# Input weights in column groups that later tensors move into, and queries stored in two parts

## The chip, the cores and the metric

One core of one Trainium2 chip runs the whole program as one launch. The metric is the device time of one execution in microseconds (us); lower is better. TensorE (PE) does matrix products, VectorE (DVE), ScalarE (ACT) and GpSimd (POOL) do elementwise work, and SyncE (SP) mostly issues DMAs. Each engine runs its own instructions in order and waits on semaphores.

## The reference

One mixer layer over 2048 new frames (16 tiles of 128) and 32 frames of a running stream (a 17th tile with 1024 cached keys), d_model 1024:

```
proj = RMSNorm(x) * g_pre @ w_in          # 2600 columns: u, gate_a, q, k, v, qi, ki, wi, gate_b
pool branch: (mean_window(u) - u) -> per-group linear -> scale, times silu(gate_a)
score = sum_h wi * relu(qi . ki)          # indexer; the 256 best visible keys of each query are kept
logits = q . k / 8 + rel_bias[bucket(distance)]; o = softmax over kept keys @ v, times silu(gate_b)
y = x + RMSNorm([pool | o] @ w_out) * g_post
```

## The kernel before, in words

The program has two phases, each one block in which every engine has its own stream, with a barrier between them. SBUF tensors of phase 1 are freed before those of phase 2 are allocated, so phase 2 loads what it needs after the barrier.

**Phase 1.** `phase1_steps` (L86) writes out one order of steps that all engines walk through. Tokens come in blocks of 4, 4, 4, 2 and 3 tiles. For each tile: N (norm of x), H (transposes into `hT`), TM (the token-major product of k, v, qi, ki, wi: 552 columns), and for each block 16 feature-major products of 128 columns each: GB (gate_b), Q, GA (gate_a), U, for four groups g. After a U come PD and PL (window means on GpSimd, difference on VectorE, a product, a VectorE multiply at L1014). TR transposes keys and index queries. I steps are pieces of the indexer scores, spread between the products; SP steps are pieces of a binary search on VectorE. The input weights `W` are one tensor [128, 8, 2600], loaded in 16 DMAs of whole row parts (L491, L493) and multiplied by g_pre on VectorE (L910) in two lots: the columns from K on when the third tile is normed, the first 1536 columns when step TM of tile 0 comes up. Three DMAs of zeros (L498) blank the end of scratch tensors in DRAM.

The relative bias is a table `G` of 8 heads (8 partitions) by 895 distances. ScalarE's queue writes it to DRAM at step TR of tile 0 (L670), 128 times over for each head, so that phase 2 can read it back with a skew as `EB` [128, 8, 768]. In phase 1 nothing but the end of the phase waits for that write (`bias_out`). ScalarE copies every product out of PSUM (fa banks 0 and 1 in turn, bank 2 for the gates, bank 3 for transposes); Q is copied with its scale and stored to `q_scratch` (L706, L563). PE needs a bank freed before it starts the product after next on it.

**Phase 2.** For each tile t, PE computes maxima products M of tile t+1 (L1473), logits A of tile t (L1486 to L1491: high part of q, low part of q, mask, shift), the weighted values two jobs behind (L1506), and the output projection O of tile t-1 (L1521: 8 products with `ma` first, then 8 with `yT`). Queries are loaded as one f32 tile (four DMAs, L1257); ScalarE rounds the high part `qh` (L1375), GpSimd subtracts to get the low part `ql` (L1315), and only then is the buffer free for the next load. ScalarE also does 16 search rounds for tile t+3 and VectorE 10 more for tile t+2, besides VectorE's maxima. SP walks its own loop over t: gb(t), mask(t+3) (tiles 3 to 5: waits for all logits of tile t), S(t+4), ma(t), q(t+2), y(t-2), xr(t-1).

Of the kernel before, what the change touches and what calls it, by code (L numbers as in the profile page):

```python
# [26 lines left out]
P = 128  # L27
D = 1024
# [19 lines left out]
COLS = 2600  # L48
BIAS_TILES = 6
# [36 lines left out]
def phase1_steps():  # L86


    steps = [("N", 0), ("N", 1), ("N", 2)]
# [34 lines left out]
    for b, (t0, nt) in enumerate(BLOCKS):  # L124
        last = b == len(BLOCKS) - 1
        ahead = [] if last else list(range(t0 + nt, t0 + nt + min(3, BLOCKS[b + 1][1])))
        todo = [(k, b, g) for g in range(NG) for k in ("GB", "Q", "GA", "U")]
        for i in range(nt):
            t = t0 + i
            if i == 0:  # L130
                for j in range(nt):
                    steps.append(("H", t0 + j))
                    spread(1)
                    seek()
                    if j == 0 and nt == 4:
                        steps.append(("N", t0 + 3))
                if last:
                    steps.append(("HIST",))
# [4 lines left out]
            project(("TM", t), 1 + sum(taking))  # L143
            pool_part()
            cached = 0 <= t - 4 < PAST // P
            for j, step in enumerate(mine):
                if step[0] != "Q":
# [3 lines left out]
                if step[0] == "U":  # L151
                    windows.append(step[1:])
                if j < 3:
# [22 lines left out]
    steps += [("NP", 0), ("NP", 1)]  # L176
# [29 lines left out]
def build(nc, A):  # L206
    ctx = ExitStack()
    with ctx:
# [8 lines left out]
        def dram(name, shape, dt=F32):  # L217
# [3 lines left out]
        q_dram = dram("q_scratch", (P, GRP, TOKENS))  # L221
# [11 lines left out]
        k2 = [sb(ctx, f"k2_{kv}", [P, SEQ], F32R) for kv in range(NKV)]  # L233
        unit = sb(ctx, "unit", [P, NT], F32)
# [4 lines left out]
        phase1(nc, A, sb, sem, identf, identb, onesb, k2, unit, banks, wide, q_dram, gb_dram, ma_dram, s_dram, m_dram,  # L239
               g_dram, k_dram)  # L240
        phase2(nc, A, sb, sem, identf, identb, onesb, k2, unit, banks, wide, q_dram, gb_dram, ma_dram, s_dram, m_dram,
               g_dram, k_dram)

# [106 lines left out]
def phase1(nc, A, sb, sem, identf, identb, onesb, k2, unit, banks, wide, q_dram, gb_dram, ma_dram, s_dram, m_dram,  # L350
           g_dram, k_dram):
# [5 lines left out]
    with ExitStack() as st:  # L357
        W = sb(st, "W", [P, DC, COLS], F32)
# [23 lines left out]
        qst = sb(st, "qst", [P, 2, 512], F32)  # L382
        U = sb(st, "U", [P, NG, UOFF + 512], F32)
# [3 lines left out]
        rows = sb(st, "rows", [HIST, 3, DPOOL], F32)  # L387
# [10 lines left out]
        wa_in = [sem(f"wa_in{c}") for c in range(DC)]  # L398
        wb_in = [sem(f"wb_in{c}") for c in range(DC)]
# [3 lines left out]
        w_scaled = sem("w_scaled")  # L403
# [13 lines left out]
        gst_out = [sem(f"gst_out{i}") for i in range(2)]  # L417
# [1277 lines left out]
```

## Time and profile before

| | us |
|---|---|
| median of 3 runs | 1875.71 (1874.71 to 1877.98) |
| the profiled execution | 1873.14 |
| its span, first to last instruction | 1871.3 |
| PE / DVE / ACT / POOL busy | 1619.6 / 1246.7 / 905.4 / 437.2 |
| granted PE clock, mean | 0.945 |

The page cuts the span into 40 slices; each digit is the busy share in tenths. Phase 1 is the first 18 to 19 slices, phase 2 the rest. A slice is 46.8 us.

```
PE   2999899979888798886487899899999999999996
DVE  3212656677676865764233899999999999885412
ACT  2112223233323334542127899888888887633331
PEclk9999899999999899988598899999999999999998
DMA  8350201020111011003712221112210110101000
```

### The profile page before, as it was taken

How to read it: one execution, taken by the hardware profiler on the slowest of the kernel's cores; microseconds unless marked ns; L12 is line 12 of the kernel's file. 1: busy time of each engine (PE TensorE's matmuls, PEld its weight loads, DVE VectorE, ACT ScalarE, POOL GpSimd, SP SyncE). 2: the span in 40 equal slices, each digit the busy share in tenths (PEclk: the TensorE clock that was granted, in tenths of full speed). 3: DMA queues.
4: the chain of work that ended last, by engine and by line, in shares of the span. 5: the costliest groups of instructions: out<-in, count | busy, mean ns of one | idle time of the engine just before them, and what ended most of it. 6: DMA issues, size and time to landing. Idle time of an engine off the chain costs nothing.

```text
span 1871.3 us, 17741 instructions
## 1 busy us (share of the span) xinstructions
PE 1619.6 (87%) x5191; PEld 892.3 (48%) x5191; DVE 1246.7 (67%) x3000; ACT 905.4 (48%) x1681; POOL 437.2 (23%) x341
## 2 busy tenths in 40 slices
PE   2999899979888798886487899899999999999996
PEld 1545555545444577664243444444444444454542
DVE  3212656677676865764233899999999999885412
ACT  2112223233323334542127899888888887633331
POOL 0000100010000101001243454434433334332342
PEclk9999899999999899988598899999999999999998
DMA  8350201020111011003712221112210110101000
GB/s 318 63 73 30 70 34 40 34 77 33 37 49 44 35 42 36 30 35 92 232 38 94 74 68 61 41 46 65 67 40 29 58 40 6 42 4 46 29 29 17
DMA packets 85587, 107.39 MB, mean 57 GB/s; under 512 B 17158, under 2 KB 64838, under 8 KB 85363
## 3 DMA queue, kind: packets, MB, share of 16 engines
q1 hardware_dynamic: 80330, 101.54, 16.3%
q10 hardware_dynamic: 5160, 4.71, 2.1%
q8 instruction: 42, 0.69, 0.2%
q14 instruction: 55, 0.44, 0.1%
HBM read 67.15 MB, written 39.09 MB: 57 GB/s over the span
## 4 chain that ended last, share of the span: by engine, by line
PE 22%; DVE 19%; issue 5%; ACT 3%; POOL 2%; DMA 1%; SPq 1%; POOLq 0%; DVEq 0%; ACTq 0%
PE wide L1521 7%; PE wide L1506 6%; DVE above L306 6%; DVE max_junk L1584 3%; DVE den L1599 2%; PE bank L1486 2%; PE bank L1487 2%; PE bank L1488 2%; POOL E L1365 2%; PE bank L1491 2%; PE bank L1473 1%; DVE S L340 1%; ACT act_junk L1415 1%; DMA q<-q_scratch 1%; DVE reach L344 1%
## 5 line engine op out<-in xcount | busy, mean ns | idle before, releaser
L785 PE MATMUL bank<-hT,W 128*128 128x512 f32 (+2 forms) x1280 | 490.2, 526 | 1.5 <-ACT kq L699 1.0
L1365 POOL TENSOR_TENSOR E<-E,EB 128x512 f32<-128x512 f32 x174 | 255.9, 1474 | 465.5 <-ACT E L1448 465.2
L785 PEld LDWEIGHTS bank<-hT,W 128*128 128x128 f32 x1280 | 243.9, 197 | 173.8 <-issue 150.7
L1448 ACT ACTIVATE E<-bank 128x512 f32<-128x512 f32 x290 | 171.7, 592 | 259.0 <-PE bank L1491 258.1
L1506 PE MATMUL wide<-E,vx 128*128 128x512 f32 x544 | 285.2, 606 | 4.0 <-POOL E L1365 4.0
L1415 ACT ACTIVATE act_junk<-S,minus_cand 128x1152 bf16<-128x1152 f32 (+9 forms) x165 | 246.3, 1493 | 2.4
L765 ACT ACTIVATE relu<-wide 128x1024 f32<-128x1024 f32 (+7 forms) x192 | 153.3, 803 | 184.5 <-PE wide L800 129.2
L1045 DVE SCALAR_TENSOR_TENSOR S<-relu,wi,S 128x1024 f32<-128x1024 f32 (+7 forms) x168 | 170.0, 1012 | 81.8 <-ACT relu L765 74.3
L1584 DVE CUSTOM_DVE_ANT_0 max_junk<-bank,mask 128x512 bf16<-128x512 f32 (+3 forms) x230 | 136.7, 613 | 103.7 <-PE bank L1473 78.3
L306 DVE TENSOR_SCALAR_CACHE_REDUCE above<-S,search 128x1152 bf16<-128x1152 f32 (+9 forms) x110 | 188.2, 1711 | 0.8
L1473 PE MATMUL bank<-k,qh 128*128 128x512 f32 (+3 forms) x214 | 143.5, 688 | 40.6 <-DVE mxp L1584 25.6
L1521 PE MATMUL wide<-wout,ma 128*128 128x512 f32 x272 | 145.6, 629 | 24.3 <-ACT osb L1441 17.0
L1486 PE MATMUL bank<-qh,k 128*128 128x512 f32 x272 | 158.4, 582 | 4.7 <-issue 2.6
L1521 PE MATMUL wide<-wout,yT 128*128 128x512 f32 x272 | 142.6, 622 | 15.4 <-POOL yT L1327 15.4
L638 POOL TENSOR_TENSOR win<-U 128x512 f32<-128x512 f32 (+11 forms) x20 | 19.0, 951 | 580.5 <-ACT U L717 580.5
L800 PE MATMUL wide<-kiT,qiT 96*128 96x512 f32 (+3 forms) x304 | 138.0, 525 | 16.2 <-ACT relu L765 16.2
L785 PE MATMUL bank<-W,hT 128*128 128x296 f32 (+1 forms) x544 | 146.2, 409 | 2.5 <-ACT hT L686 2.5
L1506 PEld LDWEIGHTS wide<-E,vx 128*128 128x128 f32 x544 | 105.0, 194 | 47.0 <-POOL E L1365 7.9
L785 PEld LDWEIGHTS bank<-W,hT 128*128 128x128 f32 x544 | 105.7, 197 | 31.1 <-issue 7.6
L1488 PE MATMUL bank<-identb,mask 128*128 128x512 bf16 x290 | 115.4, 398 | 0.0
L1491 PE MATMUL bank<-shift,onesb 128*128 128x512 bf16 x290 | 112.5, 388 | 0.0
L1487 PE MATMUL bank<-ql,k 128*128 128x512 f32 x272 | 109.6, 403 | 0.0
(183 smaller groups left out, 2128.7 us busy)
## 6 DMA issues: line engine op xcount, KB each, us to landing
q<-q_scratch SPq DMA_DIRECT2D x68, 128.0 KB, 2.9
xs<-x_prompt SPq DMA_DIRECT2D x16, 512.0 KB, 4.2
xr<-x_prompt SPq DMA_DIRECT2D x16, 512.0 KB, 5.3
y_prompt<-osb SPq DMA_DIRECT2D x16, 512.0 KB, 3.6
W<-w_in SPq DMA_DIRECT2D x8, 768.0 KB, 17.5
s_scratch<-S SPq DMA_DIRECT2D x11, 512.0 KB, 2.6
gb<-gb_scratch SPq DMA_DIRECT2D x17, 256.0 KB, 5.5
ma<-ma_scratch SPq DMA_DIRECT2D x17, 256.0 KB, 4.8
```

What stands on the lines that cost most here:

```text
L306: dve.tensor_scalar((B.above, B.reach)[i][:, 0:s.shape[1]], s, B.cand[:, i:i + 1], None, ALU.is_ge, ALU.add, accum_out=B.cnt[:, i:i + 1]). ...
L765: act.activation(relu[:, k % 2, 0:b - a], wide[k % 2][:, 0:b - a], ACT.Relu)\
L785: mm = pe.matmul(out, stationary(c), moving(c), start=(c == 0), stop=(c == DC - 1))
L1045: dve.scalar_tensor_tensor(row, relu[:, k % 2, 0:b - a], w, row, ALU.mult, ALU.add)\
L1365: pool.tensor_tensor(E[:, k % 4], E[:, k % 4], EB[:, kv * GRP:(kv + 1) * GRP, off:off + P], ALU.mult)\
L1415: act.activation(act_junk[:, 0:w], S[:, sslot(u), 0:w], ACT.Sign, bias=minus_cand[:, u % 2:u % 2 + 1], accum_out=act_sum[:])\
L1448: act.activation(E[:, k % 4], banks[2 + k % 2][:].rearrange("p (j n) -> p j n", j=GRP), ACT.Exp).then_inc(fl_free, 1)
L1473: pe.matmul(max_banks[k % 3][:, 0:b - a], qh[:, t % 2, kv, j, :], keys[:, a:b], start=True, stop=True)\
L1486: pe.matmul(bank, keys, qh[:, t % 2, kv], start=True, stop=False)
L1506: pe.matmul(wide[0][:, kv * 512:(kv + 1) * 512], values[:, kt, kv:kv + 2, :].rearrange("p a d -> p (a d)"), E[:, k % 4].rearrange("p j n - ...
L1521: mm = pe.matmul(wide[1][:, 0:512], stat, wout[:, c, i * 512:(i + 1) * 512], start=(c == 0), stop=(c == DC - 1))
L1584: dve.tensor_tensor_reduce(junk[:, k % 2, 0:b - a], max_banks[k % 3][:, 0:b - a], mask[:, t % 3, a:b], 1.0, LEAST, ALU.add, ALU.max, mxp[: ...
```

## The change

It has these parts.

1. `w_in` is laid out by the host as 16 column groups of 128 columns (each [128 partitions, 8 x 128]) and one group TM of 552 columns. On chip they lie in one tensor `home`, which both phases share. Loads: x(0), small tables, TM in 8 DMAs with x(1) between, x(2), 16 group DMAs of 512 KB with x(3) after the second. g_pre is applied to TM right after the norm of tile 0 (step WT), and to each group by one tensor-tensor multiply (step WG), one after each H of block 0 and two ahead of each product.
2. TM of tile 0 comes right behind H of tile 0, ahead of H of tiles 1 to 3.
3. `G` has no tensor of its own: it lies in `sga`, the buffer of the gate_a results. So ScalarE's first GA step waits for the write of `G` to DRAM.
4. Q: ScalarE writes the rounded high part, VectorE the low part (`qlow`), and both are stored. The bank is freed by VectorE; ScalarE waits for that before its next fa copy.
5. In the last block the order of products is U and GA of all groups first, then GB and Q. As groups of `home` are used up, `EB`, `vx`, the first `S` and half of `w_out` are loaded into them while phase 1 still runs. The NP steps move up behind the last block's first GB.
6. Phase 2 loads high and low parts as they are (eight DMAs a tile, three and two buffers), and ScalarE's and GpSimd's query steps are gone. SP's loop for t from 1 on is: gb(t), mask(t+3), high(t+2), low(t+1), and at t = 1 g_post and two S tiles, then S(t+4), ma(t) and the rest.

```diff
-    steps = [("N", 0), ("N", 1), ("N", 2)]
+    steps = [("N", 0), ("WT",), ("N", 1), ("N", 2)]
...
                     steps.append(("H", t0 + j))
+                    if b == 0 and j == 0:
+                        project(("TM", 0), 0)
...
+                    if b == 0:
+                        scale(1)
...
             for j, step in enumerate(mine):
+                scale(2)
...
-        G = sb(st, "G", [NH, GLEN], F32)
+        G = sga[:].rearrange("p a n -> p (a n)")[0:NH, 0:GLEN]
...
+                    elif s == ("Q", last_block, 2):
+                        sp.wait_ge(fa_full, fa["Q", last_block, 1] + 1)
+                        sp.wait_ge(fg_full, fg["GB", last_block, 1] + 1)
+                        sp.dma_start(home[:, 8 * GROUP:12 * GROUP], A["w_out"][:, 0:4 * GROUP])\
+                          .then_inc(loaded["wout_in"], 16)
...
                             dst = sga[:, m % 2, 0:T]
+                            if m == 0:
+                                act.wait_ge(bias_out, 16)
...
-                        act.activation(qst[:, n % 2, 0:T], banks[k % 2][:, 0:T], ACT.Copy, scale=ATTN_SCALE)\
-                           .then_inc(fa_free, 1)
+                        act.activation(qst[:, n % 2, 0:T].bitcast(F32R), banks[k % 2][:, 0:T], ACT.Copy, scale=ATTN_SCALE)\
+                           .then_inc(q_high, 1)
...
+                    elif s[0] == "WG":
+                        k = scaled_at[s[1:]]
+                        group = WG[s[1:]]
+                        dve.wait_ge(wg_in[k - 1], 16)
+                        dve.tensor_tensor(group, group, gpre[:].rearrange("p (c n) -> p c n", n=1)
+                                          .broadcast_to([P, DC, P]), ALU.mult).then_inc(wg_scaled, 1)
...
+                    elif s[0] == "Q":
+                        k, n_q, T = fa[s], q_slot[s], width(s[1])
+                        dve.wait_ge(q_high, n_q + 1)
+                        if n_q:
+                            dve.wait_ge(qlow_out, 16 * n_q)
+                        dve.scalar_tensor_tensor(qlow[:, 0:T], banks[k % 2][:, 0:T], ATTN_SCALE,
+                                                 qst[:, n_q % 2, 0:T], ALU.mult, ALU.subtract).then_inc(fa_free, 1)
...
                     load_mask(t + 3)
+                    if t >= 1:
+                        load_high(t + 2)
+                        load_low(t + 1)
+                    if t == 1:
+                        sp.dma_start(gpost[:], A["g_post"].broadcast_to([P, D])).then_inc(gpost_in, 16)
+                        load_S(FIRST + 1)
+                        load_S(FIRST + 2)
```

## Rows read from the trace of the kernel before

**Rows 1.** Windows: us, then busy us (count) by engine, PEclk, DMA share, GB/s.
```profile
20.00:40.00 20.00, 2.54 (x11) 1.74 (x9) 9.03 (x24) 0.95 (x2) 0.00 (x0) 1.00 1.01 362
60.00:80.00 20.00, 20.00 (x56) 9.39 (x55) 3.87 (x14) 4.39 (x10) 0.00 (x0) 1.00 0.43 55
...
900.00:920.00 20.00, 8.79 (x19) 4.63 (x20) 4.72 (x25) 2.14 (x3) 4.84 (x3) 0.50 1.04 352
1070.00:1110.00 40.00, 35.97 (x106) 17.13 (x105) 38.71 (x90) 36.81 (x79) 19.20 (x14) 0.96 0.28 83
```

**Rows 2.** Timeline of the start: start us, us, engine, line, what.
```profile
3.36 0.42 SPq L488 DMA_DIRECT2D relb<-rel_bias  x1
...
18.63 1.94 PE L818 MATMUL bank<-identf,xs 128*128 128x128 f32 x8 [6.79 <-DVE xs L930]
...
23.97 5.55 DVE L910 TENSOR_SCALAR W<-W,gpre 128x1064 f32<-128x1064 f32 x8
...
47.79 7.68 PE L785 MATMUL bank<-W,hT 128*128 128x256 f32 x32 [0.78 <-ACT hT L686]
...
55.31 7.03 PE L785 MATMUL bank<-hT,W 128*128 128x512 f32 x16
```

**Rows 3.** Timeline, the bias table's write and the tanh ahead of it.
```profile
62.37 0.60 ACT L733 ACTIVATE gst<-bank 128x512 f32<-128x512 f32 x1 [6.45 <-PE bank L785]
62.38 1.28 ACTq L670 DMA_DIRECT2D bias_scratch<-G  x1
```

**Rows 4.** DMA queues: packets, MB, share of 16 engines, in 64:66, 66:68, 140:141.
```profile
q10 hardware_dynamic: 27, 0.10, 46.0%
...
q10 hardware_dynamic: 29, 0.10, 49.4%
...
q10 hardware_dynamic: 1, 0.00, 0.1%
```

**Rows 5.** DMA issues in 60:150: what, count, KB each, us to landing.
```profile
gb_scratch<-gst SPq DMA_DIRECT2D x3, 256.0 KB, 22.7
```

**Rows 6.** Timeline, ScalarE's copies after U of block 0 and in TM of tile 1.
```profile
84.18 0.60 ACT L717 ACTIVATE U<-bank 128x512 f32<-128x512 f32 x1 [6.23 <-PE bank L785]
...
87.64 0.38 ACT L699 ACTIVATE kq<-bank 128x256 f32<-128x256 f32 x1 [2.86 <-PE bank L785]
```

**Rows 7.** Waits of PE, 60:870: who for whom, us in total, times, longest.
```profile
PE bank L860 <- DVE gst L1014: 35.2, 14, 5.9
```

**Rows 8.** Timeline of the end of phase 1.
```profile
862.10 7.92 PE L785 MATMUL bank<-hT,W 128*128 128x288 f32 x32
...
875.99 0.35 SPq L557 DMA_DIRECT2D ma_scratch<-gst  x1
878.61 2.58 SPq L1257 DMA_DIRECT2D q<-q_scratch  x4
```

**Rows 9.** Waits in 868:950, in total.
```profile
ACT qh L1375 <- DMA q<-q_scratch: 43.5, 3, 17.7
```

**Rows 10.** Timeline of the start of phase 2.
```profile
889.38 0.69 PE L1473 MATMUL bank<-k,qh 128*128 128x128 f32 x2 [14.04 <-ACT qh L1375]
...
919.29 2.04 PE L1521 MATMUL wide<-wout,ma 128*128 128x512 f32 x2 [7.22 <-DMA ma<-ma_scratch]
...
948.32 0.33 SPq L1248 DMA_DIRECT2D mask<-mask_scratch  x1
...
953.73 0.79 PE L1486 MATMUL bank<-qh,k 128*128 128x512 f32 x1
...
957.45 1.10 PE L1521 MATMUL wide<-wout,ma 128*128 128x512 f32 x2 [1.38 <-ACT osb L1441]
```

**Rows 11.** One line's durations: ns min/median/max, first to last start.
```profile
L1315 POOL TENSOR_TENSOR ql<-q,qh x17: 2335/2353/2368, 889.4 to 1757.9; 128x1024 fp32r<-128x1024 f32 x17
...
L1594 DVE TENSOR_SCALAR shift<-identb,nmax x136: 240/249/1325, 892.6 to 1774.4; 128x128 bf16<-128x128 bf16 x136
...
L996 DVE SCALAR_TENSOR_TENSOR gst<-gst,bank x4: 687/687/689, 63.0 to 176.7; 128x512 f32<-128x512 f32 x4
```

More of the change, by code:

```diff
@@ L48 @@
 COLS = 2600
+BASE = {"GB": C_GB, "Q": C_Q, "GA": C_GA, "U": C_U}
+FIRST_ORDER = [(kind, g) for g in range(4) for kind in ("GB", "Q", "GA", "U")]
+LAST_ORDER = [(kind, g) for g in range(4) for kind in ("U", "GA")] + [(kind, g) for g in range(4) for kind in ("GB", "Q")]
+GROUP = DC * P
+TMW = C_GB - C_K
 BIAS_TILES = 6
@@ L86, in phase1_steps, with scale @@
 def phase1_steps():
-    steps = [("N", 0), ("N", 1), ("N", 2)]
+    steps = [("N", 0), ("WT",), ("N", 1), ("N", 2)]
+    unscaled = list(FIRST_ORDER)
+    def scale(n):
+        while unscaled and n:
+            steps.append(("WG", *unscaled.pop(0)))
+            n -= 1
     inside = {}
@@ L126, in phase1_steps @@
         ahead = [] if last else list(range(t0 + nt, t0 + nt + min(3, BLOCKS[b + 1][1])))
-        todo = [(k, b, g) for g in range(NG) for k in ("GB", "Q", "GA", "U")]
+        todo = [(k, b, g) for k, g in (LAST_ORDER if last else FIRST_ORDER)]
         for i in range(nt):
@@ L218, in dram @@
             return nc.dram_tensor(name, shape, dt, kind="Internal").ap()
-        q_dram = dram("q_scratch", (P, GRP, TOKENS))
+        q_dram = [dram(f"q_{part}_scratch", (P, GRP, TOKENS)) for part in ("high", "low")]
         gb_dram = dram("gb_scratch", (P, GRP, TOKENS))
@@ L347, in choose, with homes, load_q_tile, phase1 @@
     return n
-def phase1(nc, A, sb, sem, identf, identb, onesb, k2, unit, banks, wide, q_dram, gb_dram, ma_dram, s_dram, m_dram,
-           g_dram, k_dram):
+def homes(home):
+    EB = home[:, 0:6 * GROUP].rearrange("p (h n) -> p h n", h=NH)
+    S0 = home[:, 6 * GROUP:8 * GROUP]
+    wout = home[:, 8 * GROUP:16 * GROUP].rearrange("p (c n) -> p c n", c=DC)
+    vx = home[:, 16 * GROUP:16 * GROUP + NPT * 3 * HD].rearrange("p (j a d) -> p j a d", j=NPT, a=3)
+    ma = home[:, 16 * GROUP + NPT * 3 * HD:16 * GROUP + NPT * 3 * HD + 2 * NG * P]\
+        .rearrange("p (i g n) -> p i g n", i=2, g=NG)
+    return EB, S0, wout, vx, ma
+def load_q_tile(sp, out, part, t, came):
+    for half in range(2):
+        for kv in range(NKV):
+            sp.dma_start(out[half * HD:(half + 1) * HD, kv], part[kv * HD:(kv + 1) * HD, :, t * P:(t + 1) * P])\
+              .then_inc(came, 16)
+def phase1(nc, A, sb, sem, identf, identb, onesb, k2, home, loaded, unit, banks, wide, q_dram, gb_dram, ma_dram,
+           s_dram, m_dram, g_dram, k_dram):
     steps, inside = phase1_steps()
@@ L437, in phase1 @@
         tm_order = {s[1]: i for i, s in enumerate(x for x in steps if x[0] == "TM")}
+        scaled_at = {part: k + 1 for k, part in enumerate(FIRST_ORDER)}
+        last_block = len(BLOCKS) - 1
         def width(b):
@@ L483, in _ @@
                 order = sorted(norm_order, key=norm_order.get)
-                for i in range(3):
-                    load_x(i, order[i])
+                load_x(0, order[0])
                 sp.dma_start(gpre[:], A["g_pre"]).then_inc(gpre_in, 16)
@@ L1387, in take_sums @@
                        .then_inc(sums_out, 1)
-                for kv in range(NKV):
-                    act.dma_start(vx[:, :, 2 * kv, :],
-                                  A["new_v_prompt"][0, 0, :, kv].rearrange("(j p) d -> p j d", p=P)).then_inc(v_in, 16)
-                high(0)
-                high(1)
                 def halved_by(t, r, part):
@@ L1453, in _ @@
                                 waiting.append((t, kv))
-                                if kv == NKV - 1 and t + 2 < NT:
-                                    high(t + 2)
                     if t == ST:
```

258 lines of the change are left out of this document (144 added, 114 removed).

## The prediction

> **What bounds the kernel now.** I read the page's slices first: PE is 87% busy and has two holes, the first slice and the 19th to 20th. The windows then give each stretch its limit. In 20 to 40 us PE works 2.5 of 20 us while the DMA engines are full at 362 GB/s; from the first products on it is full (20.00 of 20); in 900 to 920 it works 8.8 of 20 at a granted clock of 0.50 under a DMA share of 1.04; and in 1070 to 1110 VectorE is busy 38.7 of 40 and leads [rows 1]. So time is lost to weights at the start and to loads behind the barrier, and those two are what this change works on. Last I looked for what reads or writes the tensors that now share a place. There the table of biases stands out: its write is issued at 62.38 and its queue, q10, is still moving packets in the microsecond from 140 to 141 [rows 3, 4]. Nothing waits for it before. In the new kernel ScalarE does.
>
> **The start.** Before, the product TM of tile 0 starts at 47.79 and the first GB at 55.31 [rows 2]. New chain, by the same durations: the small table `relb` is issued behind one x tile, not three (two issues of 0.45 and 1 MB less ahead of it at some 360 GB/s [rows 1]), so everything up to the transposes of tile 0, which started at 18.63, comes 3.5 us earlier: 15.1. The eight TM scalings of 552 columns take half of the 5.55 for 1064 [rows 2], 2.9: 18.0. TM's 2.26 MB and two x tiles are 3.3 MB, 9 us of stream, landed by 14. TM of tile 0 takes 7.5 (47.79 to 55.31): 25.4. Then come VectorE's splits, the norm of tile 3 (2.8) and three rounds of transposes at 1.94 and a copy each, some 8 us together: the first GB starts at 33.3, 22.0 earlier. Its weights came long before and the scaling (16 multiplies at about 1.2, my estimate from 0.687 for 512 columns [rows 11]) runs ahead of PE. Up to here the change gains 22.
>
> **The new wait.** GB ends 22.0 earlier, so ScalarE issues the table's write at 40.4 instead of 62.38. Its rate is 27 packets in 2 us beside other stores and 29 alone [rows 4], 1024 rows of 3.6 KB in all: 71 to 76 us, and measured 77.8 from issue to the last packet. The share of 46 to 49% says eight of the sixteen engines carry it. It ends at 118.2. ScalarE reaches its first GA tanh at 54.5 and stands there, in order, with the copies of U and of TM of tile 1 behind it. PE runs on through U of group 0 and the first half of TM (to about 65.5) and then needs U's bank. After 118.2 come the tanh, a transposed copy and U's copy, 0.6 each [rows 3, 6]: PE goes on at 120.0 with TM's second half, which it started at 87.6 before [rows 6]. That is 32.4 late. PE has then idled 54 us; behind such a hole the clock was 0.50 for a while [rows 1], and I add 2.5 for half rate over some 5 us. **Start and wait together: +35.** The bounds are a write of 73 or 80 us and the first GB 3 us off: +28 to +41. The x tile for tile 4 queues behind the blanking and beside the table's packets (stores there took 22.7 to land [rows 5]), so it may come as late as 90; ScalarE is held anyway until 118. Were it later than 107, up to 11 would be added.
>
> The Trainium skill ("DMA: Bandwidth & Descriptors", Rules for kernel authors) says that an outermost dimension of fewer than 16 confines a DMA to that many engines at most. The table has 8 heads outermost and the trace agrees (46 to 49% of sixteen). By that rule nothing in the new layout speeds the write up; on all sixteen engines it would be 39 us shorter, and the forecast would be a gain.
>
> **Queries split in phase 1.** 20 VectorE subtracts: 12 at 0.69 and 8 shorter ones at about 0.45, 11.9 us in all [rows 11]. Until 190 us PE is full and they are hidden. After that PE waits for VectorE 14 times at a tile's transposes, 35.2 in all [rows 7], and there up to one subtract each can show. Both ends: 0 and 12; the bank that a Q now holds longer has 7 us of product between, so I take **+4**. The multiplies by g_pre are hidden by the stall.
>
> **The end of phase 1.** Before, the last product ends at 870.0 (862.10 + 7.92), and window, difference, product, multiply and store follow until 878.61 [rows 8], 8.6 us. Now a Q is last: copy 0.4, subtract 0.5, two issues 0.8, landing 1.7, barrier 0.9, some 4.8 with handovers. That is **-3.5**; the early loads (6.5 MB) run under the score pieces, and only the half of `w_out` can lie in front of the last store: -5 to +1.
>
> **The start of phase 2.** Let 0 be SP's first instruction, 878.61 before. The first maxima started at 10.8 (889.38) because ScalarE waited for the queries [rows 9, 10]; four DMAs at 0.64 and 2.8 of landing give 5.4. With no query step on ScalarE the first exponentials are not held up, and by the same durations the maxima of tile 1 end at 17.4, tile 1's logits start at 19.3. The first output product waited for `ma` until 919.29, at 40.7 [rows 10]; now 7.2 MB of that queue are loaded already, `ma` is issued at 17 behind 2.5 MB and is there at 22. From there to the end of tile 1's logits the work is the same chain, 26 us. That end was at 69.7 (mask issue 948.32 [rows 10]); now it is at 48: a gain of 21.5. Then something new is late. SP's mask for tile 4 waits for just this moment, and high(3) and low(2) are queued behind it: 0.3 + 2.6 + 2.6 of issue and 2.8 of landing, 8.3, where PE wants the low part after 5.4 (953.73); and `ma`, behind g_post and two S tiles, 13 to 14 us after, where it was wanted after 9.1 (957.45). That costs 4.5, and the same order for mask 5 costs 2 more one tile on. **-15**, between -8 (the waits twice as long) and -22 (no new wait).
>
> **The rest of phase 2.** ScalarE loses 17 roundings of 1.05, GpSimd 17 subtracts of 2.35 [rows 11]. VectorE leads here, and neither was in front of it in most tiles. But VectorE's 0.25 us shift rows reach 1.33 in places [rows 11], which I read as waiting for GpSimd. With some 0.5 us back in each of 12 tiles: **-6**; ends 0 and -28 (12 subtracts whole).
>
> **Sum** against the profiled execution: 1873.1 + 35 + 4 - 3.5 - 15 - 6 = 1887.6. The median is 2.6 above that execution, so I say 1889.
>
> **The rivals.**
> *VectorE gets GpSimd's time back* (ends faster). Each subtract that goes frees VectorE for its whole 2.35 us in the 12 tiles that it leads: -28 instead of -6, 1867. For: the rows of 1.33 against 0.25. Against: most shift rows are at the median, and a subtract need not meet a VectorE instruction that is kept out. It decides from 10 us beyond my 6 on, 1.3 us a tile.
> The Trainium skill ("SBUF — State Buffer", Who interferes with whom) calls the port pair of VectorE and GpSimd an exclusive lock, the later one blocked for a whole instruction. By that rule a tile could give back up to 2.35 us, the price above; the trace shows single rows five times their median, not that every subtract does it.
> *The wait costs nothing*: the write ends before ScalarE gets there, or PE finds other work. Then 22 us are gained at the start: 1873.1 - 22 + 4 - 3.5 - 15 - 6 = 1831, 1833 on the median. Against: the write would have to take 14 us, and PE's order is fixed.
> *VectorE is late in phase 1*: a subtract behind search rounds holds the bank, ScalarE's next copy waits for it and PE for that, at most of the 14 waits: +12 to +20 instead of +4, 1901. For: 5.9 us of such a wait once [rows 7]. Against: 7 us of product between.
> *The handover gives nothing*: new waits for low parts and `ma` eat the gain in phase 2: -3 instead of -15, 1901.
>
> **Chances.** Forecast 0.68, freed VectorE 0.10, no wait 0.08, late subtracts 0.08, no handover gain 0.06. The forecast's own range is 1877 to 1900. The range over all is 1867 to 1904: it leaves out the no-wait case and the tails. A difference of 0.2%, 3.7 us, is about what can be told from none. Faster: 0.08 + 0.08 + 0.02 of the forecast's tail = 0.18; the same: 0.01 + 0.07 = 0.08; slower 0.74.
>
> **What would show it.** The first 512-column product near 33; ScalarE idle from 55 to about 118 with the table's write as what ends it, and PE idle from 65 to 120; TM of tile 1 ending 33 to 36 later than at 91.4; that lag growing by under 8 until the last block; first maxima 5 to 6 us after SP's first instruction in phase 2; PE held at the first logits of tiles 2 and 3. I am wrong if ScalarE's wait ends before 100 or is absent, if the lag at 200 us is under 25, or if phase 2 is not 14 to 30 us shorter.

## The result, and the profile after

The changed kernel takes 1910.33 us (median of 4 runs, 1906.58 to 1912.48) against 1876.45 us (1874.71 to 1877.98) for the kernel before beside it: ratio 1.0187, 95% interval 1.0167 to 1.0207. It is slower, as forecast, but by 33.9 us and not 13, and outside the range that I gave (up to 1904). The profiled execution took 1908.91 us, 35.8 more than the one of before. Below, every ratio is to the kernel before, run beside that version, with a 95% interval in brackets. One execution of run 9 (1872.94 us) fell in a slower state than that kernel's others and is not counted.

The windows of the changed kernel (us, busy us and count of each engine, granted clock, DMA share, GB/s). Read them against [rows 1].

```profile
20.00:40.00 20.00, 16.54 (x60) 11.55 (x59) 14.22 (x45) 5.09 (x10) 0.00 (x0) 0.84 1.04 392
40.00:60.00 20.00, 20.00 (x52) 8.95 (x50) 1.12 (x2) 1.20 (x4) 0.00 (x0) 0.99 0.71 152
60.00:80.00 20.00, 13.45 (x37) 7.48 (x36) 7.63 (x17) 2.11 (x4) 0.00 (x0) 0.83 0.53 94
80.00:120.00 40.00, 0.00 (x0) 0.00 (x0) 0.00 (x0) 0.00 (x0) 0.00 (x0) 0.56 0.48 56
```

In 20 to 40 PE now works 16.5 of 20 us, where it worked 2.5. In 80 to 120 no engine does anything, while the DMA engines are 48% busy. The timeline of PE and ScalarE there, where [rows 2], [rows 3] and [rows 6] stood:

```profile
18.96 9.88 PE L890 MATMUL bank<-home,hT 128*128 128x256 f32 x32 [1.30 <-DVE home L1031]
...
36.42 9.10 PE L890 MATMUL bank<-hT,home 128*128 128x512 f32 x16 [0.78 <-ACT hT L786]
...
64.00 1.06 ACT L777 ACTIVATE junk<-xs 128x1024 bf16<-128x1024 f32 x1 [16.51 <-DMA xs<-x_prompt]
...
122.47 0.60 ACT L838 ACTIVATE sga<-bank 128x512 f32<-128x512 f32 x1 [56.36 <-DMA bias_scratch<-sga]
...
124.08 6.76 PE L890 MATMUL bank<-home,hT 128*128 128x296 f32 x16 [44.50 <-ACT U L820]
```

The first 512-column product starts at 36.42 instead of 55.31, and takes 9.10 us instead of 7.03 at a granted clock of 0.50 in 36 to 40 (the level of 1.2 GHz). The TM product of tile 0 takes 9.88 instead of 7.68. The windows print a clock of 1.00 there, but its first ten matmuls start 0.43 us apart and the next ones of the same width 0.22, so it too began at half the rate. ScalarE then stands 56.36 us before its first GA tanh, until the table has been written: issued at 45.57, waited for until 122.5, 76.9 us. Then it copies U and frees PE, which starts the second half of TM of tile 1 at 124.08 after 44.5 us of idleness. ScalarE's copy of the first half follows at 123.91, 36.3 later than at 87.64 [rows 6].

The last block of phase 1, rows of VectorE and then of PE:

```profile
877.37 1.22 DVE L1160 TENSOR_REDUCE small<-S 128x1 f32<-128x1024 f32 x1
878.51 1.21 DVE L1161 TENSOR_REDUCE small<-S 128x1 f32<-128x1024 f32 x1
...
880.32 0.51 DVE L1123 SCALAR_TENSOR_TENSOR gst<-bank,pscale,sga 128x288 f32<-128x288 f32 x1
```
```profile
880.88 1.03 PE L987 MATMUL bank<-identf,U 128*15 128x128 f32 x4 [4.79 <-DVE gst L1123]
...
884.50 1.09 PE L959 MATMUL bank<-identf,qs 128*96 128x128 f32 x4 [0.77 <-DVE rows L1089]
```

PE waits here for VectorE's multiply of step PL (L1123), which stands behind the sums and reductions of the indexer scores, and for the row copies of the NP steps (L1089). Over the whole last block its waits for that multiply add up to 19.3 us; in the kernel before they are 11.1. And the handover to phase 2, where [rows 8] and [rows 10] stood (the first row is SP's queue, the others PE; the last two views are PE's waits in 930 to 1060 and one row of the next tile):

```profile
933.55 2.57 SPq L390 DMA_DIRECT2D qh<-q_high_scratch  x4
```
```profile
938.40 0.69 PE L1560 MATMUL bank<-k,qh 128*128 128x128 f32 x2 [9.79 <-DMA qh<-q_high_scratch]
...
958.95 2.04 PE L1609 MATMUL wide<-home 128*128 128x512 f32 x2 [3.46 <-DMA home<-ma_scratch]
```
```profile
PE bank L1573 <- DMA ql<-q_low_scratch: 7.3, 2, 4.5
...
1038.58 0.79 PE L1573 MATMUL bank<-qh,k 128*128 128x512 f32 x1 [4.54 <-DMA ql<-q_low_scratch]
```

The first maxima start 4.85 us after SP's first instruction of phase 2, and PE then waits for low parts of the queries, which nothing did before.

To find where the 35.8 us go I follow one instruction per tile through both traces (VectorE's scaling of `wi` in TM of each tile, its reciprocal of each tile in phase 2) and take the lag, after less before:

```
TM of tile 1   tile 8   tile 14   tile 15   last product   SP phase 2   reciprocal 3   reciprocal 14   end
+39.3          +38.7    +43.9     +51.1     +58.6          +54.9        +49.8          +36.9           +35.8
```

| term | forecast | measured |
|---|---|---|
| start and wait | +35 | +39.3 |
| phase 1 from tile 1 to 14 | +4 (the split, whole phase) | +4.6 |
| last block of phase 1 | in the +4 | +14.7 |
| end of phase 1 | -3.5 | -3.7 |
| start of phase 2 | -15 | -5.1 |
| rest of phase 2 | -6 | -14.0 |

### The profile page after: what moved, and what is told of

The parts are those of the page before. It is cut to its first block, busy times and chain, and to the rows that moved or that the text cites. A ratio compares the mean times of both kernels' runs of the same rounds, so it can differ in the third digit from the quotient of the medians.

```text
span 1907.1 us, 17837 instructions
## 1 busy us (share of the span) xinstructions
PE 1624.9 (85%) x5143; PEld 897.3 (47%) x5191; DVE 1250.3 (66%) x3028; ACT 889.3 (47%) x1664; POOL 404.3 (21%) x324
## 3 DMA queue, kind: packets, MB, share of 16 engines
q10 hardware_dynamic: 1032, 3.67, 1.7%
## 4 chain that ended last, share of the span: by engine, by line
PE 20%; DVE 17%; issue 4%; ACT 4%; POOL 2%; another core or an unknown queue 2%; SPq 1%; DMA 0%; POOLq 0%; DVEq 0%; ACTq 0%
PE wide L1593 6%; PE wide L1609 6%; DVE above L329 5%; DVE max_junk L1672 3%; PE bank L1573 2%; PE bank L1575 2%; PE bank L1574 2%; ACT act_junk L1504 2%; DVE den L1687 1%; PE bank L1578 1%; POOL E L1466 1%; PE bank L1560 1%; SPq L390 1%; DVE reach L367 1%
## 5 line engine op out<-in xcount | busy, mean ns | idle before, releaser
L890 PE MATMUL bank<-hT,home 128*128 128x512 f32 (+2 forms) x1280 | 498.7, 534 | 6.9 <-DVE sga L1098 4.8
L1466 POOL TENSOR_TENSOR E<-E,home 128x512 f32<-128x512 f32 x174 | 256.7, 1479 | 497.6 <-ACT E L1537 497.5
L890 PEld LDWEIGHTS bank<-hT,home 128*128 128x128 f32 x1280 | 247.2, 200 | 184.4 <-issue 160.4
L1593 PE MATMUL wide<-E,home 128*128 128x512 f32 x544 | 282.4, 601 | 6.8 <-POOL E L1466 4.2
L890 PE MATMUL bank<-home,hT 128*128 128x296 f32 (+1 forms) x544 | 150.6, 418 | 47.5 <-ACT U L820 44.5
L1609 PE MATMUL wide<-home 128*128 128x512 f32 x272 | 144.8, 626 | 22.5 <-ACT osb L1530 15.4
L1504 ACT ACTIVATE act_junk<-S,minus_cand 128x1152 bf16<-128x1152 f32 (+5 forms) x105 | 155.3, 1479 | 1.4
L1609 PE MATMUL wide<-home,yT 128*128 128x512 f32 x272 | 139.7, 611 | 15.9 <-POOL yT L1432 15.9
L890 PEld LDWEIGHTS bank<-home,hT 128*128 128x128 f32 x544 | 108.1, 202 | 77.9 <-ACT U L820 44.9
L329 DVE TENSOR_SCALAR_CACHE_REDUCE above<-S,search 128x1152 bf16<-128x1152 f32 (+5 forms) x70 | 118.6, 1694 | 0.5
```

The source lines that it names most:

```text
L329: dve.tensor_scalar((B.above, B.reach)[i][:, 0:s.shape[1]], s, B.cand[:, i:i + 1], None, ALU.is_ge, ALU.add, accum_out=B.cnt[:, i:i + 1]). ...
L890: mm = pe.matmul(out, stationary(c), moving(c), start=(c == 0), stop=(c == DC - 1))
L1466: pool.tensor_tensor(E[:, k % 4], E[:, k % 4], EB[:, kv * GRP:(kv + 1) * GRP, off:off + P], ALU.mult)\
L1504: act.activation(act_junk[:, 0:w], S[sslot(u)][:, 0:w], ACT.Sign, bias=minus_cand[:, u % 2:u % 2 + 1], accum_out=act_sum[:])\
L1593: pe.matmul(wide[0][:, kv * 512:(kv + 1) * 512], values[:, kt, kv:kv + 2, :].rearrange("p a d -> p (a d)"), E[:, k % 4].rearrange("p j n - ...
L1609: mm = pe.matmul(wide[1][:, 0:512], stat, wout[:, c, i * 512:(i + 1) * 512], start=(c == 0), stop=(c == DC - 1))
```

## The experiments

Lags are against the profiled kernel before, as above.

**1. The table in a tensor of its own** (no wait is needed then):

```diff
-        G = sga[:].rearrange("p a n -> p (a n)")[0:NH, 0:GLEN]
+        G = sb(st, "G", [NH, GLEN], F32)
...
-                            if m == 0:
-                                act.wait_ge(bias_out, 16)
```

> The changed kernel with the bias table in a tensor of its own again, and without ScalarE's wait before the first GA. Theory (the shared place costs the stall): PE no longer stops from 80 to 124 us. The trace of the changed kernel shows another, shorter hold that stays: ScalarE waits until 64.0 for the x tile of tile 4, PE for that from 60.0 to 66.2. So TM of tile 1 should start its second half near 78 instead of 124.1, 46 us earlier, and the total falls from 1910 to 1862 to 1866. Rival (stores and loads slowed by the write would hold the engines nearly as long): less than half of it, over 1888.

Measured: 1852.74 us (1850.71 to 1863.58), ratio 0.9896 (0.9866 to 0.9926), a gain of 57.6 on the changed kernel and faster than the kernel before. TM of tile 1 lags -17.1 instead of +39.3. PE and ScalarE at the same place:

```profile
59.81 0.60 ACT L836 ACTIVATE sga<-bank 128x512 f32<-128x512 f32 x1 [6.23 <-PE bank L888]
```
```profile
60.05 7.03 PE L888 MATMUL bank<-hT,home 128*128 128x512 f32 x16
66.92 7.60 PE L888 MATMUL bank<-home,hT 128*128 128x256 f32 x32
```

Without the shared place tile 1 is 56.4 us earlier: the table's wait decides the sign of the whole change. That is some 10 more than I expected. The x tile of tile 4 landed at 48.6 here and at 64.0 in the changed kernel, so PE did not stand its 6 us for it. Run 10, further down, has no wait either and its x tile landed at 63.8; it lags -8.4 at tile 1. So with a late x tile the wait is worth 47.7 us, about what I expected, and the other 9 come from the x tile's landing, which runs 9 and 12 come back to.

**2. The table's write in eight DMAs, one per head.** The prediction had priced this at 39 us by a rule of the Trainium skill ("DMA: Bandwidth & Descriptors", Rules for kernel authors).

```diff
-                        act.dma_start(g_dram, G.rearrange("h (a n) -> h a n", a=1).broadcast_to([NH, P, GLEN]))\
-                           .then_inc(bias_out, 16)
+                        for h in range(NH):
+                            act.dma_start(g_dram[h:h + 1], G[h:h + 1].rearrange("h (a n) -> h a n", a=1)
+                                          .broadcast_to([1, P, GLEN])).then_inc(bias_out, 16)
```

> The changed kernel with the table's write issued as 8 DMAs, one per head, so that 128 copies and not 8 heads are outermost. The wait stays. Theory (eight engines carry the one DMA, 0.53 us a row each): all sixteen take part, the write takes about 40 us instead of 77, the wait ends near 86 instead of 122.5, total 1873 to 1877. Rival (reading rows of one partition is what limits it, whichever engines do it): the write takes as long or longer, total 1905 or more.

Measured: 1966.69 us (1965.21 to 1971.2), ratio 1.0496 (1.048 to 1.0513), 56 us slower than the changed kernel. The queue's line in 44 to 190, and ScalarE's tanh:

```profile
q10 hardware_dynamic: 1152, 3.67, 81.7%
```
```profile
179.34 0.60 ACT L839 ACTIVATE sga<-bank 128x512 f32<-128x512 f32 x1 [39.59 <-DMA bias_scratch<-sga]
```

All sixteen engines carry it (81.7% of the sixteen, the same 3.67 MB), and it takes 1.7 times as long: 27 GB/s instead of 48. In the changed kernel 1032 packets took 40.8% of sixteen engines over 80 us, 0.51 us each; here 1152 took 81.7% over 146 us, 1.66 us each. Spreading each row's copies over more engines gained nothing and made each packet three times as long. The engines are confined as that rule says, but my sentence that on all sixteen the write would be 39 us shorter is wrong. What holds the packets back (the source partition, or the order in which a DMA's packets are dealt out) these runs don't tell.

**3. The NP steps at the end again:**

```diff
-                if step == ("GB", len(BLOCKS) - 1, 0):
-                    steps += [("NP", 0), ("NP", 1)]
...
     spread(100)
+    steps += [("NP", 0), ("NP", 1)]
```

> The changed kernel with the two NP steps at the end of phase 1 again. In the trace of the changed kernel they sit between GB and Q of the last block: PE waits 4.8 us for VectorE's multiply, then two round trips over VectorE until 884.5. If they cost what they show there, 3 to 5 us go and some 2 come back at the end: 1906 to 1909. If the 14.7 us that the last block lost are mainly theirs, 1900 or less. If the multiply behind the score reductions is the real hold, the transposes of index queries wait for it in their place and nothing moves: 1910.

Measured: 1908.1 us (1904.09 to 1908.47), ratio 1.0173 (1.0156 to 1.019). The first maxima lag +45.0 instead of +49.0, but reciprocal 16 +36.3, where the changed kernel has +37.0. The steps' new place costs 4 us in phase 1. They are still there at reciprocal 3 (+45.8 against +49.8) and are lost between tiles 3 and 14, where this edit changes nothing: PE is busy there for 630.6 us at a mean granted clock of 0.98, in the changed kernel for 625.3 at 0.99. The clock is enough to swallow the 4 us; no run takes this apart.

**4. Low and high parts of the queries ahead of the masks in SP's loop of phase 2:**

```diff
-                    load_mask(t + 3)
                     if t >= 1:
-                        load_high(t + 2)
                         load_low(t + 1)
+                        load_high(t + 2)
+                    load_mask(t + 3)
```

> The changed kernel with the loads of low and high parts ahead of the mask load in SP's loop in phase 2. Theory (low parts queued behind the masks of tiles 4 and 5 hold PE, and with them ma): the lag against the kernel before grew by 8.3 us from the first to the second reciprocal and by 2.5 to the third; 4 to 8 of these go, total 1902 to 1906. Rival (the growth comes from the output products waiting for ma behind g_post and two S tiles, which stays as it is): 1908 or more.

Measured: 1896.19 us (1891.15 to 1900.7), ratio 1.0115 (1.0091 to 1.0139): 14.1 us faster than the changed kernel on the median, 17.8 in the profile, more than forecast. The waits for `ql` are gone from PE's list in 930 to 1060; what is left there of loads behind the first is this:

```profile
PE wide L1609 <- DMA home<-ma_scratch: 4.3, 2, 2.5
```

Reciprocal 3 lags +30.1 instead of +49.8. The new waits of the handover, which I had priced at 6.5, were worth 17.6 (at reciprocal 14) to 19.7 (at reciprocal 3) in these profiles. The run also turns the order of high and low parts around, so it prices both together. The rows named for them add up to 7.3 only: a late tile also moves its masks, whose loads wait for its last logits, so the loss is passed on, as I read it; no run takes this apart further.

**5 and 6. Early loads late; and the first order in the last block.** Run 5 is run 3 with the four early loads behind the last step of phase 1; run 6 is run 5 with the last block in the order of all others.

```diff
                         sp.dma_start(dst, src).then_inc(gst_out[n % 2], 16)
-                        early_loads(s)
...
                         sp.dma_start(q_dram[1][:, j, a:a + width(b)], qlow[:, 0:width(b)]).then_inc(qlow_out, 16)
-                        early_loads(s)
...
+                for part in (("GB", last_block, 0), ("GB", last_block, 1), ("Q", last_block, 1), ("Q", last_block, 2)):
+                    early_loads(part)
                 sp.wait_ge(m_out, 16 * len(EARLY))
```
```diff
-        todo = [(k, b, g) for k, g in (LAST_ORDER if last else FIRST_ORDER)]
+        todo = [(k, b, g) for k, g in FIRST_ORDER]
```

> The changed kernel with the four early loads (biases, values, the first S tile, half of w_out: 6.5 MB) issued behind the last step of phase 1 instead of inside its last block, and the two NP steps at the end; the last block's new order stays. Theory A (the order of the last block costs there): the first query product's neighbours stay as late as in the run with NP at the end, TM of tile 16 lags 47 behind the kernel before, and the first maxima of phase 2 lag 45 plus some 15 more, because 6.5 MB now stand in the queue ahead of the queries; end 1915 to 1925 us. Theory B (the early loads take the last block's time, by their waits on SP or their bytes): TM of tile 16 lags 36 to 40 only, and the last product ends 8 to 10 us earlier than in the changed kernel; end 1905 to 1915.

> As the run with late loads, and besides the last block runs in the order of the kernel before (GB, Q, GA, U of each group) instead of U and GA first. Theory A: the lag stays under 42 through the last block, TM of tile 16 lags 40 and not 47, the last product ends some 12 us earlier than with the new order, and the whole is 8 to 12 us faster than the run with late loads. Rival (the last block's loss comes from the split of the queries or from slower clock after the table's hole): no difference of more than 3 us between the two.

Measured: run 5 1920.83 us (1920.29 to 1922.88), ratio 1.0254 (1.0236 to 1.0272); run 6 1915.76 us (1913.94 to 1915.87), ratio 1.0223 (1.0205 to 1.024).

```
lag            TM of tile 14   tile 15   tile 16   first maxima   end
run 3          +43.1           +50.3     +47.2     +45.0          +36.3
run 5          +43.9           +51.1     +48.0     +63.3          +51.2
run 6          +41.8           +42.3     +40.9     +53.3          +42.3
```

The last column is reciprocal 16. The jump of 7.2 between tile 14 and 15 is in run 5 as in run 3, so it is not the early loads; with the first order it is gone. At the last product run 5 lags +55.0 and run 6 +41.2; 2.1 of that difference was there at tile 14 already, so in the last block the order costs 11.8. The NP steps cost 3.6 there (+14.7 in the changed kernel, +11.1 in run 3). The first order gives some 4 of it back at the handover, because U with its window, product and multiply is last again (the -3.5 of the forecast): at the first maxima 10.0 are left, 8 of them the order's. Theory A holds in phase 1, though run 6's median gains 5.1 on run 5 and not 8 to 12. PE's waits in 780 to 930, run 5 and then run 6:

```profile
PE bank L963 <- DVE gst L1122: 10.2, 2, 6.5
PE bank L958 <- DVE gst L1122: 9.0, 2, 4.8
```
```profile
PE bank L959 <- DVE gst L1123: 6.8, 1, 6.8
...
PE bank L964 <- DVE gst L1123: 4.6, 1, 4.6
```

Run 5 against run 3 prices the early loads: 18.3 us at the first maxima, 14.9 at the end. Of run 6 against run 5 the profiles show 8.9 us at the end and the medians 5.1: the profiled execution is the slowest of run 5's four and the fastest of run 6's.

**7. Runs 1 and 4 together:**

> The changed kernel with the table of biases in a tensor of its own and no wait at the first GA tanh (alone 1852.7 us), and with the low parts and high parts of the queries issued ahead of the masks in SP's loop of phase 2 (alone 14 to 19 us faster than the changed kernel). If the two are independent, the sum holds: 1834 to 1839 us. Rival (the low parts' gain is slack that a lead in phase 1 also takes): 1845 or more.

Measured: 1840.35 us (1836.67 to 1852.9), ratio 0.9845 (0.9805 to 0.9885). The sum of the two nearly holds (1838.6), and 1840.35 is just above the range that I gave. The low parts are worth 12.4 us on the medians here, against run 1, and 13.9 at reciprocal 16.

**8. GpSimd's work back, in four short instructions a tile:**

```diff
+                            if 2 <= t + 1 < NT:
+                                for i4 in range(4):
+                                    pool.wait_ge(spare_done, 4 * (t - 1) + i4 + 1)
+                                    pool.tensor_tensor(spare[:], spare[:], spare[:], ALU.subtract)\
+                                        .then_inc(spare_done, 1)
```

> As the run before it, and GpSimd does 15 times, where the kernel before had its query subtract in phase 2, four subtracts of 256 columns on a spare tensor (some 2.4 us a tile together): the work that the change took from GpSimd is given back and nothing else. Theory of the prediction (GpSimd's instructions keep VectorE out now and then, half a microsecond a tile): slower than the run before it by 3 to 8 us, and VectorE's shortest rows of phase 2 show more outliers. Rival 1 (an exclusive port, every subtract costs VectorE its length): slower by 20 to 30. Rival 2 (what phase 2 gained over my forecast came from ScalarE's roundings or from the clock): within 2.

Measured: 1843.62 us (1841.76 to 1853.78), 3.3 more than run 7, 5.5 in the profile. That is at the low end of my theory, and less than the executions of either run scatter (12 and 16 us), so it can't be told from nothing. The lag against the kernel before still fell by 10.5 from reciprocal 7 to 14, as in run 7 (10.6), so most of phase 2's gain was elsewhere, or the shape mattered.

**10. ScalarE's roundings back,** two copies of 512 columns a tile:

```diff
                                 waiting.append((t, kv))
+                                if kv == NKV - 1 and t + 2 < NT:
+                                    act.wait_ge(qh_in[(t + 2) % 3], 64 * ((t + 2) // 3 + 1))
+                                    for half in range(2):
...
+                                        act.activation(spare[:], qh[:, (t + 2) % 3, half].bitcast(F32)
+                                                       .rearrange("p j n -> p (j n)"), ACT.Copy).then_inc(spare_done, 1)
```

> The run with the table of its own and low parts ahead of masks (1840.4 us), with the rounding of the queries that the change took from ScalarE in phase 2 put back as two copies of 512 columns on a spare tensor per tile, at the place where the kernel before had it (some 1.2 us a tile, 15 tiles). Theory (the 12 us that phase 2 gains between tiles 7 and 14, 1.8 a tile, are this work, because ScalarE's exponentials and copies of sums release PE there): 8 to 18 us slower, 1849 to 1858, and the lag against the kernel before falls no more from tile 7 to 14. Rival (ScalarE has slack in every tile, and the gain is in VectorE's or PE's own rows): within 3 us of 1840.

Measured: 1842.76 us (1833.94 to 1859.18). From the first maxima to the end it gains 28.4 us on the kernel before, run 7 gains 25.7. From reciprocal 7 to 14 the lag falls by 11.4, as without them. My theory falls: ScalarE's roundings cost nothing that these runs show.

**11. One long GpSimd instruction a tile.** What sent me there is a pair of rows of the kernel before that I had not read for the prediction:

```profile
1529.77 2.36 POOL L1315 TENSOR_TENSOR ql<-q,qh 128x1024 fp32r<-128x1024 f32 x1
...
1530.88 1.27 DVE L313 SCALAR_TENSOR_TENSOR search<-search,search 128x1 f32<-128x1 f32 x1
```

The update of the search takes 1.27 us where its median is 0.16, and ends at 1532.15 with GpSimd's subtract (1532.13). In 960 to 1760 the kernel before has 29 such rows more than 0.5 above their median, the changed one 16. Each of them ends within 0.06 us of the end of a GpSimd instruction. In the kernel before 8 of the 29 end with a subtract of the queries, among them the longest (2.07 us), and these 8 are together 11.5 us over the median; 20 end with instructions of 512 columns (1.3 us) and one with the residual's addition, the kinds that the changed kernel still has (15 and one).

```diff
                     pool.wait_ge(post_done, t + 1)
+                    if t + 3 < NT:
+                        both = osb[0:r, t % 2, :]
+                        pool.tensor_tensor(both, both, xr[0:r, :], ALU.add).then_inc(held, 1)
+                        pool.wait_ge(held, t + 1)
```

> The run with the table of its own and low parts ahead of masks (1840.4 us), with one GpSimd addition of 1024 columns more in each of 14 tiles of phase 2, beside the place where the kernel before had its query subtract: the same length of one instruction, not four short ones. It adds the residual a second time (the output is that much off). Theory (a long GpSimd instruction keeps a VectorE instruction with two SBUF operands out until it ends; in the kernel before 29 search rows took 0.7 to 1.5 us instead of 0.16, together 28 us in 12 tiles, after the change 16 of them): the count of such rows goes back towards 29 and the run is 8 to 13 us slower than 1840. Rival (four short ones cost 3 us, and a long one no more than that): 1840 to 1845, rows unchanged.

Measured: 1855.65 us (1847.54 to 1868.54), ratio 0.9911 (0.988 to 0.9941). The search's group of VectorE in 1100 to 1740 (busy us, mean ns | idle before), of the changed kernel, of run 8 and of run 11:

```profile
L336 DVE SCALAR_TENSOR_TENSOR search<-search,search 128x1 f32<-128x1 f32 x105 | 33.5, 319 | 3.6
```
```profile
L336 DVE SCALAR_TENSOR_TENSOR search<-search,search 128x1 f32<-128x1 f32 x90 | 30.4, 338 | 3.1
```
```profile
L336 DVE SCALAR_TENSOR_TENSOR search<-search,search 128x1 f32<-128x1 f32 x93 | 42.5, 457 | 3.2
```

457 ns is what the kernel before had (455), and there are 26 long rows, of which 8 end with the added instruction. The lag, which fell by 10.6 and 10.5 from reciprocal 7 to 14 in runs 7 and 8, is now flat: -5.0 at reciprocal 3, -4.5 at 7, -4.6 at 14. One long instruction gives back the whole slope, four short ones of the same sum and at the same place, behind the residual, do not. The updates alone are enough to account for it. From reciprocal 3 to reciprocal 14 each kernel has 107 of them:

```
                 updates, us   the whole stretch, us
kernel before    49.8          691.1
changed kernel   33.9          678.2
run 7            34.6          680.3
run 8            38.0          683.9
run 11           47.3          691.5
```

VectorE's other large groups there agree within 1 us between the kernel before and the changed one, and no wait of PE in run 11 ends with the residual, which the added instruction delays. The 3.4 us more in run 8 are no more than chance shows: run 10, without any work given back to GpSimd, has updates of 37.1 in a stretch of 676.7. The 15 us on run 11's median are no clean price of that instruction, the 10 to 11 of the slope are: in its profile the start alone is 17.6 us later than in run 7 (TM of tile 1 lagged +0.2, not -17.4: its x tile again, which landed at 71.9 and held PE 15.5 us).

**9 and 12. The best of it.** Run 9 adds to run 7 the first order in the last block, with the groups' places in the big tensor in that order too, so that the early loads can stay early (each behind the groups whose place it takes; NP as in run 3). Run 12 also loads the x tile of tile 4 ahead of the blanking DMAs.

```diff
-              for i, part in enumerate(LAST_ORDER)}
+              for i, part in enumerate(FIRST_ORDER)}
...
-                    sp.dma_start(home[:, i * GROUP:(i + 1) * GROUP], A["w_in"][:, i * GROUP:(i + 1) * GROUP])\
+                    sp.dma_start(home[:, k * GROUP:(k + 1) * GROUP], A["w_in"][:, i * GROUP:(i + 1) * GROUP])\
```
```diff
+                load_x(4, order[4])
                 sp.wait_ge(blank, 1)
...
-                        if s[1] and taken < NT:
+                        if s[1] > 1 and taken < NT:
```

> The run with the table of its own and low parts ahead of masks (1840.4 us), and the last block of phase 1 in the order of the other blocks (GB, Q, GA, U), with the groups' places in the big tensor in that same order, so that the biases, values, first S tile and half of w_out can still be loaded inside the last block; the NP steps at the end. Theory (the order alone cost 9 to 10 us in the last block, and the early loads don't need it): 1829 to 1834 us, and a lag of TM of tile 15 that stays within 2 of that of tile 14. Rival (the order is what lets the early loads land in time; later loads stand in the queries' way): the first maxima gain less than 4, 1837 or more.

> The run with the last block in the first order (1839.1 us, from 1826.5 to 1872.9), and the x tile of tile 4 and three small loads issued ahead of the blanking DMAs. Theory (in kernels without the wait for the table the start hangs on when that x tile lands, 56 us in one run and 66 in two others, which moved everything behind it by 9 to 11 us): it lands by 45, TM of tile 1 lags -17 or less in the profiled run, times scatter less, and the median is 1824 to 1832 us. Rival (SP, held until tile 1 is transposed before it may load this tile, delays blanking and stores, and PE waits for those): 1836 or more.

Measured: run 9 1839.1 us (1826.51 to 1852.31), ratio 0.9812 (0.9771 to 0.9853); run 12 1830.07 us (1824.06 to 1835.26), ratio 0.9767 (0.9742 to 0.9792), the fastest version here. From TM of tile 1 to the first maxima run 7 loses 8.0 us and run 9 gains 2.4, so order and NP steps together are worth 10.4 in phase 1. By its median run 9 missed its range (1829 to 1834), because its start fell badly; ScalarE in run 9 and in run 12:

```profile
66.19 1.06 ACT L776 ACTIVATE junk<-xs 128x1024 bf16<-128x1024 f32 x1 [20.32 <-DMA xs<-x_prompt]
```
```profile
47.05 1.06 ACT L777 ACTIVATE junk<-xs 128x1024 bf16<-128x1024 f32 x1
```

This x tile is issued on SP's queue within a microsecond or two of the table's write on ScalarE's, and when it lands goes with which of the two comes first (profiled executions, in order of the first column):

```
run                        1      8      5      7      changed   10     4      3      9      11
x issued after table, us   -0.5   -0.1   +0.0   +0.5   +0.7      +0.7   +0.8   +0.9   +1.0   +1.7
x landed at, us            48.6   49.7   49.6   56.4   64.0      63.8   66.6   67.3   66.2   71.9
```

The blanking had landed by 44.5 in all of these, so it is the table's packets that the tile stands behind, as I read it. Run 6, which issues it 9.8 us behind, gets it at 81.5. In run 9 it held PE 10.0 us. Run 12 issues it 7.7 us ahead of the table; it lands at 44.1, nobody waits for it, and the times of run 12 lie within 11 us, where the five of run 9 lie 26 apart. Only the profiled executions can be read this way, so that the scatter of the others has the same cause is likely and not shown.

## Why the forecast had the sign right and the size wrong

In the profiles the kernel is 21.3 us slower than the sum said. The start is 4.3 of it, phase 1 behind it 15.3, the start of phase 2 9.9; the end of phase 1 gives 0.2 and the rest of phase 2 8.0 back. The sign rests on the start and wait alone, and that term was sound.

*Start and wait, +35 against +39.3: right.* The three things that it rested on are there: first 512-column product near 33 (36.4), ScalarE held until about 118 (122.5), the write as long as before (76.9 us against 77.8). The 4 us are the slower first two products (2.2 and 2.1 us), which I had left out. PE idled 44.5 us in the hole and not 54, but it had stood 6.1 for the x tile of tile 4 before. That changed nothing: in run 5 the tile landed at 49.6, and the lag at tile 1 is the same (+39.4).

*Queries split in phase 1, +4: the first step that failed is that it stood for the whole of phase 1.* The changed order of the last block had no term of its own. I read the diff's order only for what it lets go early, and took PE to be full behind it. In fact U and GA first put all PL multiplies and the NP copies in front of the transposes that PE needs, and on VectorE these stand behind the sums and reductions of the scores. The runs put some 12 us on the order and 4 on the NP steps, together the block's 14.7 within 1. For tiles 1 to 14 the number agrees (+4.6), but not by the mechanism that I gave: in the changed kernel no engine's wait ends with a subtract of the low parts, and PE's waits for the multiply add up to 28.2 us in 200 to 784, as in 160 to 740 of the kernel before. No run takes the split out, so what the 4.6 are stays open, and that +4 fits them is luck as far as is known.

*End of phase 1, -3.5: right (-3.7).*

*Start of phase 2, -15 against -5.1: the gain was right in size, the new waits, the second step that failed, were mis-sized.* From SP's first instruction of phase 2 to reciprocal 3 run 4 gains 23.7 us on the kernel before, where I had 21.5 without new waits; run 5 puts 14.9 to 18.3 on the early loads. The low parts and `ma` behind the masks I priced at 6.5; the changed kernel loses 18.6 to run 4 in the same stretch. The mechanism and the order on SP's queue were the right ones. What I left out is that a late tile makes its masks and the loads behind them late too, so that the wait is paid again in the tiles behind; that reading is argued and not tested apart.

*Rest of phase 2, -6 against -14.0: the right mechanism, too small, and the wrong row to size it by.* I took the size from outliers of the shift rows and not from the search's update, which has the long rows. GpSimd's subtract is 10 to 11 of it: 8 updates held for 1.4 us each, where I had 12 tiles at 0.5. The other 3 no run explains; kernels with the same work in phase 2 differ by as much behind reciprocal 3. The Trainium skill ("SBUF — State Buffer", Who interferes with whom) calls the port pair an exclusive lock: the engine that comes first holds it for its whole instruction and the other is blocked until then. The trace agrees in kind: all 29 long rows end with a GpSimd instruction, the longest after 2.07 us. As a price the rule's upper end (2.35 us a tile) is too much: on average 0.8 us a tile came back, because the update falls somewhere within the subtract, and not in every tile.

Of the rivals, the freed VectorE was half true and beside the point, since the miss in the last block was larger. VectorE late in phase 1 (1901, 0.08) was the nearest in place and size: VectorE's multiply, late behind the scores' reductions, did hold a bank, but through the order, not through the subtracts of the split.

## What to carry over

Before a tensor moves into another's place, find the last reader of the old content and ask when it ends; if it is a DMA, measure that DMA. Here it read for 77 us, and the shared place cost 48 to 56 us, more than the whole change brings at its best (43 us, run 12 against the kernel before). Give an order that is changed for the sake of early loads a term of its own: list what each engine finds in front of PE's next need. A wait in a chain of loads that wait for each other's consumers can cost more than the rows that name it (7.3 us named, 14 to 20 paid). Where an engine waits for another's instruction now and then, look for the rows that end together, in every group of the engine, before sizing the wait.

## What the runs showed of the hardware

A DMA that writes 128 copies of 8 rows of one partition each took 77 us (48 GB/s) on eight engines and, cut into eight DMAs over sixteen, some 135 us (issued from 44.2 on, done at 179; 27 GB/s), with 1.66 us a packet against 0.51. More engines were slower.

A load of 512 KB issued up to half a microsecond ahead of that write landed in about 4 us; issued 0.7 to 1.7 us behind it, within 18 to 26.

A VectorE instruction of one element per partition (scalar-tensor-tensor with both inputs in SBUF, 0.16 us at the median) took up to 2.07 us beside a GpSimd instruction of 2.36 us, and ended with it. A tensor-scalar instruction of the same shape (`side` of the search) beside it never took more than 0.16. The length of one GpSimd instruction matters here, not the sum: one of 1024 columns cost 10 to 11 us over 14 tiles, four of 256 columns at the same place 3.3 us at most on the median, which is within the scatter.
